# First and last row fetches of the second table moved, and the pairs of row products started four blocks sooner

## The reference

```python
def block(args):
    tb, ib, gb = args                 # tokens, indices of experts, weights
    ue = u_tab[ib]
    act = jax.nn.gelu(jnp.einsum("phkd,pd->phk", ue, tb))
    ve = v_tab[ib]
    return jnp.einsum("phk,phkd->pd", gb * act, ve)
...
h = h + peer(rmsnorm(h, norm2_g[l]), peer_wq[l], peer_subkeys[l], peer_u[l], peer_v[l])
```

## Time and profile before

| | us |
|---|---|
| executions | 1604.69, 1608.52, 1608.29 |
| median | 1608.29 |
| the profiled execution: device time | 1607.7 |
| the profiled execution: span, first to last instruction | 1605.9 |
| PE busy in the span | 1582.2 |
| third stage (blocks 0 to 127 of `v_tab`), about | 641.6 to 969.7 |

### The profile page before, as it was taken

The page is one execution under the profiler, slowest core; times in us unless marked ns, Lnnn a source line. Parts: engine busy times, 40 slices in busy tenths (PEclk is TensorE's granted clock), DMA queues, the critical chain, the costliest instruction groups (busy, mean ns, idle before and its releaser), DMA issues.

```text
span 1605.9 us, 28383 instructions
## 1 busy us (share of the span) xinstructions
PE 1582.2 (99%) x9931; PEld 1382.6 (86%) x9931; DVE 1251.1 (78%) x2489; ACT 923.7 (58%) x1686; POOL 468.0 (29%) x337
## 2 busy tenths in 40 slices
PE   9999999999999999999999999999999999999998
PEld 8999899999988888777777777988888888788886
DVE  7888879878987777677777777778777877687777
ACT  5766655555466665555555555675555546555554
POOL 1000001888778762455554550110000000000000
PEclk9999999999999999999999999999999999999999
DMA  7766756777777776899999996346556653455653
GB/s 241 234 234 228 253 178 197 186 183 192 190 187 184 184 184 195 285 335 333 338 339 338 368 375 200 126 136 196 188 183 193 197 175 128 132 183 183 195 186 104
DMA packets 126226, 347.95 MB, mean 217 GB/s; under 512 B 34992, under 2 KB 40752, under 8 KB 125744
## 3 DMA queue, kind: packets, MB, share of 16 engines
q1 hardware_dynamic: 87408, 294.93, 55.7%
q0 software_dynamic: 32000, 42.06, 10.0%
q10 hardware_dynamic: 6720, 9.65, 1.8%
HBM read 331.31 MB, written 14.75 MB: 215 GB/s over the span
## 4 chain that ended last, share of the span: by engine, by line
PE 84%; issue 7%; DVE 4%; DMA 2%; ACT 1%; POOL 0%; SPq 0%; POOLq 0%; DVEq 0%; ACTq 0%
PE ps L1451 17%; PE ps L1433 9%; PE ps L1434 9%; PE ps L1435 9%; PE ps L1453 8%; PE ps L1496 7%; PE ps L1617 7%; PE ps L1498 6%; PE ps L1500 6%; PE ps L1633 2%; DMA raw<-in_v_tab 1%; PE ps L1608 1%; PE ps L1467 1%; DVE low L1944 1%; DVE held_low L1944 1%
## 5 line engine op out<-in xcount | busy, mean ns | idle before, releaser
L1944 DVE TENSOR_TENSOR low<-raw,high 128x1024 fp32r<-128x1024 f32 (+1 forms) x516 | 622.4, 1211 | 149.0 <-ACT high L990 133.1
L990 ACT ACTIVATE high<-raw 128x1024 fp32r<-128x1024 f32 (+1 forms) x517 | 539.0, 1046 | 290.4 <-PE ps L1435 123.9
L1451 PE MATMUL ps<-x_parts,high 128*128 128x512 f32 x1184 | 420.1, 398 | 0.0
L1433 PE MATMUL ps<-x_parts,low 128*128 128x256 f32 x1328 | 377.9, 285 | 0.9 <-DVE x_parts L2063 0.9
L1435 PE MATMUL ps<-x_parts,high 128*128 128x256 f32 x1328 | 375.7, 283 | 0.0
L1434 PE MATMUL ps<-x_parts,high 128*128 128x256 f32 x1328 | 375.7, 283 | 0.0
L1453 PE MATMUL ps<-x_parts,low 128*128 128x256 f32 x1184 | 331.7, 280 | 0.0
L875 POOL DMA_INDIRECT routed<-h_tok,subln x128 | 267.2, 2088 | 138.2 <-DVE h_tok L2329 67.9
L1451 PEld LDWEIGHTS ps<-x_parts,high 128*128 128x128 f32 x1184 | 222.4, 188 | 52.6
L1433 PEld LDWEIGHTS ps<-x_parts,low 128*128 128x128 f32 x1328 | 254.8, 192 | 2.7 <-issue 1.3
L1434 PEld LDWEIGHTS ps<-x_parts,high 128*128 128x128 f32 x1328 | 254.8, 192 | 0.0
(11 more groups left out here) (389 smaller groups left out, 2163.2 us busy)
## 6 DMA issues: line engine op xcount, KB each, us to landing
raw<-in_u_tab SPq DMA_DIRECT2D x128, 512.0 KB
raw<-in_v_tab SPq DMA_DIRECT2D x128, 512.0 KB
raw<-in_ffn_in SPq DMA_DIRECT2D x88, 512.0 KB
raw<-in_w_mix SPq DMA_DIRECT2D x56, 512.0 KB
raw<-in_ffn_out SPq DMA_DIRECT2D x44, 512.0 KB
routed<-arena POOLq DMA_DIRECT2D x16, 512.0 KB, 4.0
raw<-in_w_query SPq DMA_DIRECT2D x16, 512.0 KB
h_tok<-routed SPq DMA_DIRECT2D x32, 256.0 KB
```

Of the source, the lines that this page charges most:

```text
L990: a.activation(w_high(p, 0, n), cols(raw, p, 0, n), ACT.Copy).then_inc(slot_high[p.slot], 1)
L1433: pe.matmul(dst, left[1], right[0], start=start, stop=False)
L1451: pe.matmul(bank(b).rearrange("p (h t) -> p h t", h=2), cols(high, p, k * PARTS, PARTS), both[:, k], start=(k == 0), stop=False)
L1944: v.tensor_tensor(w_low(p, 0, n), cols(raw, p, 0, n), w_high(p, 0, n).bitcast(F32), ALU.subtract).then_inc(slot_low[p.slot], 1)
```

## The change

1. The first four row fetches (pairs 0 and 1) no longer stand ahead of the wait for the dump of activations. They stand behind the activations' fetches and both coefficients, and each waits for one more count of `coef_ready`: 3, 5, 7 and 9.
2. The double pairs stand behind blocks 8, 16, ... 120, which makes 15 of them.
3. Pairs 30 and 31 use the ordinary buffers and windows. Their fetches wait for the products of pairs 28 and 29, which now come behind block 120. Both pairs are multiplied behind the last block, ahead of the transposes of tile 0.
4. DVE's `add_rest` is cut in halves, each followed by its part of the split, and it waits for all 32 pairs instead of 30. ACT takes the high part of the fourth block behind the last one (`diff_v` 3) after the sum of squares instead of before it. DVE keeps its place for the low part.

```diff
-            for n in range(2):
-                gather_rows(n)
             pool.wait_ge(dumped, 16 * NKEYS // DUMP)
             for n in range(2):
                 gather_acts(n)
-            pool.memset(late_windows, 0.0).then_inc(pool_ready, 1)
-            pool.wait_ge(pool_ready, 3)
+            pool.wait_ge(pool_ready, 2)
             for n in range(2):
                 coefficients(n)
+            for n in range(2):
+                gather_rows(n, 3 + 2 * PACE * n)
             for n in range(PAIRED - 2):
                 pool.wait_ge(c_ready, n + 1)
                 gather_acts(n + 2)
-                if n + 2 < PAIRED - LATE_PAIRS:
-                    pool.wait_ge(pair_mixed, n + 1)
-                    gather_rows(n + 2)
+                pool.wait_ge(pair_mixed, n + 1)
+                gather_rows(n + 2)
                 coefficients(n + 2)
-                if n in (20, 24):
-                    gather_rows(PAIRED - LATE_PAIRS + (n - 20) // 4)
...
+                    if paced is not None:
+                        pool.wait_ge(coef_ready, paced + PACE * t)
...
-            after = {12 + 8 * m: (2 * m, 2 * m + 1) for m in range((PAIRED - LATE_PAIRS) // 2 - 1)}
+            after = {FIRST + 8 * m: (2 * m, 2 * m + 1) for m in range(PAIRED // 2 - 1)}
...
-            for n in range(PAIRED - LATE_PAIRS - 2, PAIRED):
-                if n == PAIRED - LATE_PAIRS:
-                    turn(h_tok, 2, (0, 1))
+            for n in range(PAIRED - 2, PAIRED):
                 rows_product(n)
+            turn(h_tok, 2, (0, 1))
...
-                ahead(piece_v(j, it))
+                if j < NKEYS - 1:
+                    ahead(piece_v(j, it))
...
-            norm(2, 2, [], False)
+            norm(2, 2, [piece_v(NKEYS - 1).later(RING)], False)
...
-            add_rest()
-            evacuate_turned(2, (0, 1))
+            v.wait_ge(c_ready, PAIRED)
+            v.wait_ge(pair_mixed, PAIRED)
+            add_rest(0)
+            evacuate_turned(2, (0,))
+            add_rest(1)
+            evacuate_turned(2, (1,))
             add_fetched()
```

More of the change, by code:

```diff
@@ L74 @@
 PAIRED = GATHERED // 2
-LATE_PAIRS = 2
 DUMP = 4
+PACE = 2
+FIRST = 8
 BODY = 8
@@ L457, in build @@
         WINDOWS, WIDE = D + PARTS + GATHERED, PAIRED - 1 + PAIRED
-        windows, late_windows = h_tok[:, WINDOWS:WINDOWS + 4 * WIDE], stage[:, 0:4 * WIDE]
-        row_homes = [v_rows[:, D * n:D * (n + 1)] for n in range(4)] + [part(18944 + D * n, D) for n in range(2)] + [part(2048 + D * n, D) for n in range(2)]
+        windows = h_tok[:, WINDOWS:WINDOWS + 4 * WIDE]
+        row_homes = [v_rows[:, D * n:D * (n + 1)] for n in range(4)]
         def row_home(n, t):
-            return row_homes[2 * (n % 2) + t if n < PAIRED - LATE_PAIRS else 4 + 2 * (n - PAIRED + LATE_PAIRS) + t]
-        def windows_of(n):
-            return windows if n < PAIRED - LATE_PAIRS else late_windows
+            return row_homes[2 * (n % 2) + t]
         def window(n, t):
             first = (2 * (n % 2) + t) * WIDE + n
-            return windows_of(n)[:, first:first + PAIRED]
+            return windows[:, first:first + PAIRED]
         def centres(n):
-            return windows_of(n).rearrange("p (n t c) -> p n t c", n=2, t=2)[:, n % 2, :, PAIRED - 1]
+            return windows.rearrange("p (n t c) -> p n t c", n=2, t=2)[:, n % 2, :, PAIRED - 1]
         def of_pair_of_tokens(t, r):
@@ L1625, in rows_product @@
                 pe.wait_ge(c_ready, n + 1)
[L1626 to L1629, removed]
+                pe.wait_ge(row_loaded[n % 2], 32 * (n // 2 + 1))
                 for t in range(2):
@@ L2415, in _, with add_rest @@
             lower, upper = slice(0, GATHERED), slice(GATHERED, PARTS)
[L2417 to L2423, removed]
-                    chain.step(v.tensor_tensor(h, h_back[upper, D + half * HALF:D + (half + 1) * HALF], bank(2 + half)[upper], ALU.add))
-                    v.wait_ge(moved_ready, 1 + half)
-                    chain.wait()
-                    v.tensor_tensor(h, h, moved[upper, half * HALF:(half + 1) * HALF], ALU.add)
+            def add_rest(half):
+                h = h_tok[upper, D + half * HALF:D + (half + 1) * HALF]
+                v.wait_ge(tile_done[1], 2 + half + 1)
+                chain.step(v.tensor_tensor(h, h_back[upper, D + half * HALF:D + (half + 1) * HALF], bank(2 + half)[upper], ALU.add))
+                v.wait_ge(moved_ready, 1 + half)
+                chain.wait()
+                v.tensor_tensor(h, h, moved[upper, half * HALF:(half + 1) * HALF], ALU.add)
             def add_fetched():
```

6 lines of the change are left out of this document (3 added, 3 removed).

## The result

| | us |
|---|---|
| before, median of 4 | 1608.39 |
| changed, median of 4 (1620.43 to 1622.48) | 1621.78 |
| ratio, 95% interval | 1.0086 [1.0075, 1.0098] |
| changed, profiled execution: device time, span | 1621.16, 1619.3 |
| forecast | 1605.0 (1601.5 to 1611.5) |

The account below looks back on a forecast made before the run. It took PE, busy 99%, as the bound, with DMA engines close behind. Head -2.3, last fetches -0.5 and behind the stage -0.5 gave -3.3 us: 1604.4 against the profiled 1607.7, median forecast 1605.0, range 1601.5 to 1611.5.

Parts of the forecast that it names:

- What bounds the kernel: Whole kernel: PE busy 99% of the span; in the third stage DMA engines 93% busy, later saturated near 400 GB/s.
- the loss at blocks 6 to 8: Head of third stage: the burst of four row fetches starves the ring; without it blocks run plain, -4.29 us.
- First fetches: Head of third stage: -4.29 us regained, a new 2.0 us wait for rows behind block 8, together -2.3 us.
- The bound from above, 9.2 us: Row fetch landing, seen at block 116 in a saturated stretch; at block 8 it would make the new loss 7.2 us.
- POOL's chain is late: Rival at block 8: dump lands as late as before, 654.60, everything 6.8 us later; +5.4 us, 1613.7; chance 0.12.
- half share: Rival before block 8: fetches beside loads get half of 399 GB/s, 3.7 us wait and clock dip; 1608.7; chance 0.25.
- The clean spread: Rival at the head: rows in time for pair 1, block 116's wait gone whole; -5.8 us, 1602.5; chance 0.2.
- Last fetches, -0.5: End of third stage: four fetches leave the stretch from 882 us; half of block 116's 0.96 us wait goes, -0.5 us.
- in time by 2 us: Behind block 120: the last rows, for pairs 30 and 31, land some 2 us before use, hidden behind blocks and held products.
- Behind the stage, -0.5: At the transposes: DVE sets the end and starts add_rest 0.5 us sooner, once PE's pairs end at 971.60; -0.5 us.
- ACT's swap: Behind the stage: taking the sum of squares before the diff_v piece lets ACT start it about 1.1 us sooner.
- Signs named ahead: Wrong if POOL's first row fetch is after 659 or before 653, clock 0.5 behind block 8 or transposes, or blocks 121-127 longer.

Follow-up runs that it names:

- e3: Kernel before with only the first four row fetches moved behind activation fetches and coefficients, with the four waits; doubles still from block 12: 1609.08 us, ratio 1.0006.
- e5: Kernel before with the first four row fetches spread behind the weighings of blocks 3, 5, 6 and 7, ahead of the dump's wait: 1606.68 us, ratio 0.9995.
- e11: Changed kernel with SyncE holding back its v_tab loads of blocks 15 and later until pair 1's rows have landed: 1617.71 us, ratio 1.0059 to the kernel before.
- e4: Kernel before with only its fourteen doubles moved, behind blocks 8 to 112 instead of 12 to 116: 1608.24 us, ratio 1.0003.
- e1: Changed kernel with the first four row fetches back at the head of POOL's list, without waits: 1612.02 us, ratio 1.0026 to the kernel before.
- e14: Kernel before, buffers and fetches kept, with pairs 30 and 31 ahead of the transposes and DVE's sum behind both, as in the changed kernel: 1607.84 us, ratio 1.0009.
- e13: Kernel before with the row fetches of pairs 30 and 31, into their own buffers, sent at the end of POOL's list: 1610.99 us, ratio 1.0027.
- e2: Changed kernel with the first double behind block 12 and the fifteen doubles spread evenly to block 120: 1613.76 us, ratio 1.0040 to the kernel before.
- e9: e1 with 8 idle matmuls on TensorE ahead of the transposes and 6 behind them: 1612.23 us, ratio 1.0027 to the kernel before.
- e8: Changed kernel with the first four row fetches spread behind the weighings of blocks 3, 5, 6 and 7, ahead of the dump's wait: 1618.04 us, ratio 1.0056.

## Why the prediction was wrong

**What bounds the kernel** was read rightly: PE without a gap, DMA engines near their limit. So was the cause of the loss at blocks 6 to 8: it was the fetches, and without them it is gone (after, e3, e5). Its size was not: 4.29 us is one execution with a dip of the clock, and three others with the same burst lose 1.0 to 1.4 there and see no dip. The term was read from a single trace; as an estimate from these four, it may be 3 us too large for most executions.

**First fetches: the step that failed.** The prediction put a new wait of 2.0 us behind block 8, from a chain on POOL in which the dump and the row fetches each land in 4.0 us. The wait measured 10.6, and the clock behind it cost 4.0. Term by term (the dump's landing and the rows' are counted to the instruction that waited for them):

| term | forecast | measured |
|---|---|---|
| last dump issued | 643.8 | 644.5 |
| its landing | 4.0 | 6.2 |
| first activation fetch to second coefficient | 8.6 | 10.5 |
| second row fetch out; fourth | 658.7; 661.2 | 664.3; 667.8 |
| from there until PE has the rows | 4.0 | 7.3; 7.7 |
| PE multiplies pair 1 at | 665.2 | 675.5 |
| clock behind it | full | 0.50, 4.0 us |

The wait for pair 1 was 10.3 us later than said. Of these, 6.6 are the chain up to the fourth fetch and 3.7 the landing. The two landings of 4.0 were medians over a whole run, taken for a stretch in which the DMA engines moved 261 to 271 GB/s and POOL's own four fetches stood behind each other. With the stream of blocks held back (e11), the rows are there in 4.5 and 4.6 us: the 4.0 was nearly right without the stream, and 3 us short beside it. The bound from above, 9.2 us, came from the same queue and from the same kind of fetch; the measured 7.3 and 7.7 are nearer to it than to 4.0. The prediction named a loss of 7.2 with it and a dip of 1.9 on top, which by its own sum is 1612.1, and set the range's end at 1611.5. The second fault: three lengths in one chain (dump, coefficients, landing) came out long together, and I ranged them one at a time. That they are long for one reason, busy DMA engines, e11 shows for the landing; for the other two it is argued.

**The rivals.** "POOL's chain is late" (0.12) named the mechanism, and "half share" (0.25) the other part; the truth is both at once, so it lies outside each. Chain late: the dump landed at 650.7, between the forecast's 647.8 and the rival's 654.6. Half share: the Trainium skill's page "DMA: Bandwidth & Descriptors", section "Queues, rings and completion order", has each engine take packets from its queues in turn. The runs agree in direction and not in size: 7.3 and 7.7 us beside the stream, 4.5 and 4.6 with it held (e11), 1.6 to 1.7 times as long and not twice. That a fetch gets just half is the prediction's reading of that rule. The clean spread, too, exists, with the doubles from block 12: e5 has it, and gains 0.05%, which is not clear of nothing, and not the 5.8 us of that rival.

**The two coupled edits.** The diff moved fetches later and their use earlier. e3 and e4 show each at nothing, e1 the pair at 9.6 us. The prediction saw both moves and had the window right (14.5 us for a chain of 8.6); the chain with the dump and the landing in it was 644.5 to 675.5, 31 us.

**Last fetches, -0.5.** The right way in the stage, and larger than said: the wait of 0.96 us is gone and the other blocks lose 1.8 us less. Pairs 30 and 31 "in time by 2 us": pair 31 came 1.00 us late.

**Behind the stage, -0.5: wrong sign, +3.2.** The prediction took the sum of squares to start 1.1 us sooner by ACT's swap. It started behind later transfers instead: its place in the order gained nothing, because what it waits for came later. The first scaling leads the third transpose by 9.67 us before (970.74 to 980.41) and by 9.89 after (983.09 to 992.98), so the order by itself costs 0.2 there; what moved is when the scaling can start. (In e14, where DVE has the scaling early and then waits for the pairs, it is 11.15.) In e1 it is 971.99, in e4 969.96, though block 124 starts at 959.6 in both. In e1 ACT waits until 965.40 and 968.92 for pieces of `diff_v`; after, DVE waits for the scaling row as well. Those transfers stand beside the rows of pairs 30 and 31, fetched from 952 to 960 in e1 and from 963 to 973 after; before, these were sent at 882 and 923, and the last ordinary fetch at 948.29. That the late rows are what delays them is read from the trace and agrees with e13's and e14's ratios, but no run moved the loads alone. By ratio the whole of this part is e1 against e4, 0.23%, 3.7 us (with the two intervals 0.03 to 0.43%). So the cause of this smaller part of the loss stays open.

**Signs named ahead.** Of the three that would make the forecast wrong, two came: the first row fetch on POOL later than 659 (661.38) and a clock of 0.5 behind block 8. Blocks 121 to 123 did not get longer.

## What to carry to other kernels

When an edit moves a transfer later and another moves its use earlier, add up the whole chain from the last event that nothing moves (here the dump's issue) to the use, and size every link by the slowest like transfer of that stretch, all together: here all three links were long at once. A wait on a counter spreads nothing if the counter has long passed; look up when each count is reached. Bytes that are moved to the end of a saturated stage land beside the next stage's first loads, so count a gain in the stage only together with what starts behind it. And before a loss that one trace shows is booked as a gain, see whether other executions have it in that size: 4.29 us here, 1.0 to 1.4 in three others.

## What had not been expected of the hardware

The length of a wait alone did not tell whether the clock would fall. Behind waits of 2.98 us (e2) and 1.87 us (e9, block 8), and behind the pair 1.00 and 1.56 at the end of the changed kernel's stage, the granted clock stayed at 1.00; behind 2.38, 3.09 (e3), and pairs of short waits with a little work between, 1.00 and 1.60 (e8) or 2.05 and 1.56 (e1), it was 0.50. The executions of e8 spread over 10 us (1611.39 to 1621.16), against 2 for the changed kernel. Only one of them has a trace, but the mean granted clock of each is on record: 0.997 in the fastest, 0.994 in the slowest. As an estimate from these, 0.003 of 1616 us is some 10 us more at half the clock, which costs at most 5: about half of the spread. The rest was not tried.
